# Group norm of the recurrence's outputs by blocks of tokens, within the rounds of the recurrence

## The reference, cut to what matters

```python
_, o = lax.scan(step, state0, (...))             # o: tokens x 8 heads x 64
mu = jnp.mean(o, axis=-1, keepdims=True)
var = jnp.mean(jnp.square(o - mu), axis=-1, keepdims=True)
o = ((o - mu) * lax.rsqrt(var + GN_EPS)).reshape(B, S, D_RWKV) * ln_x_g + ln_x_b
bonus = jnp.sum(rh * kh * r_k, axis=-1, keepdims=True) * vh
o = o + bonus.reshape(B, S, D_RWKV)
return o * g                                     # g = sigmoid(zg) @ w_gate_up
...
mix = jnp.concatenate([attn, rw], axis=-1) @ w_out
x = x + rms_norm(mix, norm_mix_post)
```

## Time and profile before

| | |
|---|---|
| median of three runs | 1931.57 us (1931.26 to 1932.75) |
| profiled execution | 1927.53 us, its span 1925.9 us |
| TensorE (PE) busy | 1806.5 us, 94%; 8894 matmuls |
| VectorE (DVE) busy | 1032.5 us, 54% |
| ScalarE (ACT) busy | 644.4 us, 33% |
| GpSimd (POOL) busy | 84.4 us, 4% |
| DMA | 210.14 MB, mean 109 GB/s |

### The profile page before, as it was taken

The page is one execution under the profiler, slowest core; times in us unless marked ns, Lnnn a source line. Parts: engine busy times, 40 slices in busy tenths (PEclk is TensorE's granted clock), DMA queues, the critical chain, the costliest instruction groups (busy, mean ns, idle before and its releaser), DMA issues. The chain is left out here.

```text
span 1925.9 us, 21538 instructions
## 1 busy us (share of the span) xinstructions
PE 1806.5 (94%) x8894; PEld 1466.7 (76%) x8894; DVE 1032.5 (54%) x1305; ACT 644.4 (33%) x807; POOL 84.4 (4%) x90
## 2 busy tenths in 40 slices
...
PEclk8669999999899899999999999996999999999999
...
GB/s 353 295 73 92 109 249 186 108 153 219 136 85 87 66 109 88 110 88 91 107 92 79 82 109 21 5 23 44 66 99 110 88 99 98 88 109 88 110 88 66
DMA packets 123954, 210.14 MB, mean 109 GB/s; under 512 B 14046, under 2 KB 48502, under 8 KB 123857
## 3 DMA queue, kind: packets, MB, share of 16 engines
...
...
HBM read 205.58 MB, written 4.73 MB: 109 GB/s over the span
## 5 line engine op out<-in xcount | busy, mean ns | idle before, releaser
L1676 DVE TENSOR_TENSOR w_lo<-raw,w_hi 128x2048 fp32r<-128x2048 f32 x138 | 316.3, 2293 | 499.9 <-ACT w_hi L1209 499.9
L1209 ACT ACTIVATE w_hi<-raw 128x2048 fp32r<-128x2048 f32 x138 | 263.8, 1913 | 612.1 <-PE bank L540 584.1
L540 PE MATMUL bank<-h_hi,w_hi 128*128 128x512 f32 x736 | 291.9, 397 | 5.1 <-DVE h_lo L1723 5.1
L540 PE MATMUL bank<-h_lo,w_hi 128*128 128x512 f32 x736 | 288.8, 392 | 0.0
L540 PE MATMUL bank<-h_hi,w_lo 128*128 128x512 f32 x736 | 288.5, 392 | 0.0
L540 PE MATMUL bank<-u_hi,w_hi 128*128 128x512 f32 x512 | 200.7, 392 | 0.0
L540 PE MATMUL bank<-u_hi,w_lo 128*128 128x512 f32 x512 | 199.4, 389 | 0.0
L540 PE MATMUL bank<-u_lo,w_hi 128*128 128x512 f32 x512 | 199.2, 389 | 0.0
L540 PE MATMUL bank<-f_hi,w_hi 128*128 128x512 f32 x496 | 193.0, 389 | 0.0
L540 PE MATMUL bank<-f_lo,w_hi 128*128 128x512 f32 x496 | 193.0, 389 | 0.0
L540 PE MATMUL bank<-f_hi,w_lo 128*128 128x512 f32 x496 | 192.9, 389 | 0.0
...
## 6 DMA issues: line engine op xcount, KB each, us to landing
raw<-in_mlp_w SPq DMA_DIRECT2D x128, 512.0 KB, 4.6
...
```

Of the source, the lines that this page charges most:

```text
L540: mm = te.matmul(bank[:, n], a, b, start=first and k == 0 and j == 0, stop=last and k == 3 and j == 2, skip_group_check=s == SLABS["ffn"] + 1)
L1209: se.activation(m.ring(s)[0], m.raw[:, slot], ACT.Copy).then_inc(sem("hi_made"), 1)
L1676: ve.tensor_tensor(lo, m.raw[:, slot], hi.bitcast(F32), ALU.subtract).then_inc(sem("lo_made"), 1)
```

## The change

The group norm is done by blocks of 128 tokens. The statistics of blocks 0, 1 and 2 are computed by VectorE in rounds 4, 6 and 7 (`O_STATS`: u = 3, 5, 6), square included. GpSimd computes (var/64 + eps)^-0.5 with a multiply-add and a power (`o_rstd`), in place of ScalarE's root and VectorE's reciprocal. In rounds 5, 7 and 8 (`O_BACK`: u = 4, 6, 7) the block is scaled, turned by TensorE (`o_back`) and gated (`o_gated`). Block 3 follows behind the rounds; its transposes stand between the first and the second token block of slab 87.

The bonus moves to round 2 (its products to round 1), the gates to round 3. The algebra is rearranged: `bonus` becomes (bonus + ln_x_b) * gate and `gT` becomes gate * ln_x_g, so that a block needs one multiplication and one addition after it has been turned. `gates()` stands on ScalarE at the end of round 3, behind the exponentials.

The transposes of x stand in round 8 as wide uses, and all eighths of `xT` are done by round 7. `x_before` lies in `kkT` and `vvT` instead of `ar`, and the squares of later norms go to `ar`. `m_hi` and `m_lo` are made by token blocks, slab 86 is split by ScalarE in round 8, and slabs 86 and 87 run one token block after the other, each waiting for its own blocks (`before_tile`). `state(7, 1)` on VectorE is removed.

```diff
-            uses += [("gate", 0), ("gate", 1), ("bonus", 0), ("bonus", 1)]
+        uses += {1: [("bonus", 0), ("bonus", 1)], 2: [("gate", 0), ("gate", 1)], 7: [("x_rows", j) for j in range(4)]}.get(u, [])
+        if u in O_BACK:
+            uses.append(("o_back", O_BACK.index(u)))
...
+O_STATS = (3, 5, 6)
+O_BACK = (4, 6, 7)
+X_FINAL = ((0,), (1,), (2,), (3,), (4, 5), (6,), (7,), ())
...
+        self.o_sq = place_s("o_sq", [P, 512])
...
+            if before_tile and k == 0:
+                before_tile(n)
...
+    def x_to_rows(j):
+        b = wide("x_rows", j)
+        te.wait_ge(sem("x_final"), DT)
+        for k in range(DT):
+            mm = te.transpose(bank[:, b + k // 4, P * (k % 4):P * (k % 4) + P], m.xT[:, k, P * j:P * j + P], ident)
+        mm.then_inc(sem("wide_full"), 1)
...
+    def o_turned(j, b):
+        te.wait_ge(sem("o_scaled"), j + 1)
+        for i in range(4):
+            mm = te.transpose(bank[:, b, P * i:P * i + P], m.o_rows[:, j].rearrange("p h d -> p (h d)")[:, P * i:P * i + P], ident)
+        return mm
...
+        if last:
+            x_to_rows(0)
+            x_to_rows(1)
...
+        if u == 1:
+            bonuses(0)
+            bonuses(1)
+        if u == 2:
             gate(0)
             gate(1)
-            bonuses(0)
-            bonuses(1)
         unit_parts(u)
         if not last:
             key_values(u + 1)
+        else:
+            x_to_rows(2)
+            x_to_rows(3)
         step(u, 0)
+        if u in O_BACK:
+            o_back(O_BACK.index(u))
...
+            def before_tile(n):
+                te.wait_ge(sem("attn_hi" if k == 0 else "o_hi"), n + 1)
+                te.wait_ge(sem("attn_lo" if k == 0 else "o_lo"), n + 1)
+            def last_turned(n):
+                if k == 1 and n == 0:
+                    o_turned(3, 4).then_inc(sem("last_o_turned"), 1)
+            slab(s + k, group, m.m_hi[:, 4 * k:4 * k + 4], m.m_lo[:, 4 * k:4 * k + 4], k == 0, k == 1, None, before_n,
+                 weights_stationary=False, after_n=None if g else last_turned, before_tile=None if g else before_tile)
...
+    def gates():
+        se.wait_ge(sem("inverses_out"), 16)
+        for part in range(2):
+            b = wide_full("gate", part)
+            se.wait_ge(sem("gate_summed"), part + 1)
+            for i in range(2):
+                ins = se.activation(m.gT[:, 2 * part + i], bank[:, b + i], ACT.Copy, scale=m.col("ln_x_g_2", 2 * part + i))
+            ins.then_inc(sem("wide_emptied_act"), 1)
+    def x_rowed(j):
+        b = wide_full("x_rows", j)
+        se.activation(m.x_before[j], bank[:, b:b + 2].rearrange("p b t -> p (b t)"), ACT.Copy).then_inc(sem("wide_emptied_act"), 1)
+    def attn_hi(n):
+        tok = slice(P * n, P * n + P)
+        se.wait_ge(sem("wide_emptied_act"), WIDE_EMPTIED[WIDE_AT["attn", n]][1])
+        se.activation(m.m_hi[:, 0:4, tok], m.attnT[:, :, tok], ACT.Copy).then_inc(sem("attn_hi"), 1)
+    def o_hi(n):
+        tok = slice(P * n, P * n + P)
+        se.wait_ge(sem("o_gated"), n + 1)
+        se.activation(m.m_hi[:, 4:8, tok], m.bonus[:, :, tok], ACT.Copy).then_inc(sem("o_hi"), 1)
...
+        if u == 2:
+            gates()
+        if last:
+            for j in range(4):
+                x_rowed(j)
+            se.wait_ge(sem("attn_summed"), UNITS)
+            split_to(SLABS["w_out"])
+            se.wait_ge(sem("unit_used"), UNITS)
+            for n in range(3):
+                attn_hi(n)
...
+    attn_hi(3)
...
+    for n in range(3):
+        o_hi(n)
+    split_to(SLABS["w_out"] + 1)
+    o_hi(3)
...
+    def bonus_made():
+        ve.wait_ge(sem("blocks_in"), 128)
+        for i in range(4):
+            ins = ve.scalar_tensor_tensor(out=m.bonus[:, i], in0=m.rT[:, i], scalar=m.col("r_k_2", i), in1=m.kkT[:, i],
+                                          op0=ALU.mult, op1=ALU.mult)
+        ins.then_inc(sem("bonus_made"), 1)
...
+    def gates():
+        ve.wait_ge(sem("wide_emptied_dve"), WIDE_EMPTIED[WIDE_AT["bonus", 1]][1])
+        for part in range(2):
+            b = wide_full("gate", part)
+            for i in (2 * part, 2 * part + 1):
+                ins = ve.scalar_tensor_tensor(out=m.bonus[:, i], in0=m.bonus[:, i], scalar=m.col("ln_x_b_2", i), in1=bank[:, b + i % 2],
+                                              op0=ALU.add, op1=ALU.mult)
+            ins.then_inc(sem("gate_summed"), 1)
...
+    def o_stats(j):
+        o, mu, var = m.o_rows[:, j], m.gs[:, 0, j], m.gs[:, 1, j]
+        sq = (m.o_sq[:, :] if j < 3 else m.ar[:, 3, 0]).rearrange("p (h d) -> p h d", h=8)
+        ve.wait_ge(sem("o_copied"), 2 * j + 2)
+        n = own.on(ve.tensor_reduce(mu, o, AX, ALU.add))
+        ve.wait_ge(own.sem, n)
+        n = own.on(ve.tensor_scalar(mu, mu, 1.0 / 64, None, ALU.mult))
+        ve.wait_ge(own.sem, n)
+        n = own.on(ve.tensor_tensor(o, o, spread8(mu), ALU.subtract))
+        ve.wait_ge(own.sem, n)
+        n = own.on(ve.tensor_tensor(sq, o, o, ALU.mult))
+        ve.wait_ge(own.sem, n)
+        ve.tensor_reduce(var, sq, AX, ALU.add).then_inc(sem("o_varied"), 1)
+    def o_scaled(j):
+        ve.wait_ge(sem("o_rstd"), j + 1)
+        ve.tensor_tensor(m.o_rows[:, j], m.o_rows[:, j], spread8(m.gs[:, 1, j]), ALU.mult).then_inc(sem("o_scaled"), 1)
+    def o_gated(j):
+        tok = slice(P * j, P * j + P)
+        ve.wait_ge(sem("wide_emptied_act"), WIDE_EMPTIED[WIDE_AT["gate", 1]][1])
+        if j < 3:
+            b = wide_full("o_back", j)
+        else:
+            b = 4
+            ve.wait_ge(sem("last_o_turned"), 1)
+        ins = ve.tensor_tensor(m.gT[:, :, tok], bank[:, b].rearrange("p (i t) -> p i t", i=4), m.gT[:, :, tok], ALU.mult)
+        if j < 3:
+            ins.then_inc(sem("wide_emptied_dve"), 1)
+            ve.wait_ge(sem("wide_emptied_dve"), WIDE_EMPTIED[WIDE_AT["o_back", j]][1])
+        else:
+            ve.wait_ge(own.sem, own.on(ins))
+        ve.tensor_tensor(m.bonus[:, :, tok], m.bonus[:, :, tok], m.gT[:, :, tok], ALU.add).then_inc(sem("o_gated"), 1)
...
+        for k in X_FINAL[u]:
+            ve.scalar_tensor_tensor(out=m.xT[:, k], in0=m.xT[:, k], scalar=m.col("final_g", k), in1=m.first_rstd,
+                                    op0=ALU.mult, op1=ALU.mult).then_inc(sem("x_final"), 1)
+        if u == 0:
+            bonus_made()
+        if u == 1:
+            bonuses()
+        if u == 2:
+            gates()
+        if u in O_BACK:
+            o_scaled(O_BACK.index(u))
+        if u in O_STATS:
+            o_stats(O_STATS.index(u))
...
+        if u in O_BACK:
+            o_gated(O_BACK.index(u))
...
+    split_to(SLABS["w_out"])
+    for n in range(3):
+        attn_lo(n)
+    o_stats(3)
+    attn_lo(3)
+    for n in range(3):
+        o_lo(n)
+    split_to(SLABS["w_out"] + 1)
+    o_scaled(3)
+    o_gated(3)
+    o_lo(3)
...
+    def o_rstd(j):
+        var = m.gs[:, 1, j]
+        ge.wait_ge(sem("o_varied"), j + 1)
+        ge.tensor_scalar(var, var, 1.0 / 64, GN_EPS, ALU.mult, ALU.add).then_inc(sem("o_meaned"), 1)
+        ge.wait_ge(sem("o_meaned"), j + 1)
+        ge.tensor_tensor(var, var, m.minus_half[:, :], ALU.pow).then_inc(sem("o_rstd"), 1)
     ge.wait_ge(sem("slab_used"), SLABS["w_out"])
     unit_scaled(0)
+    ge.memset(m.minus_half[:, :], -0.5).then_inc(sem("half_set"), 1)
+    ge.wait_ge(sem("half_set"), 1)
     for u in range(1, UNITS):
         unit_scaled(u)
+        if u - 1 in O_STATS:
+            o_rstd(O_STATS.index(u - 1))
+    o_rstd(3)
```

More of the change, by code:

```diff
@@ L518, in emptied, with slab @@
         te.wait_ge(sem(f"{engine}_emptied"), count)
-    def slab(s, group, hi, lo, first, last, before_k=None, before_n=None, weights_stationary=True, k_outer=False, after_n=None):
+    def slab(s, group, hi, lo, first, last, before_k=None, before_n=None, weights_stationary=True, k_outer=False, after_n=None, before_tile=None):
         w_hi, w_lo = m.ring(s)
@@ L1547, in scalar_program @@
             exps(u + 1, (2, 3))
-        else:
-            for part in range(2):
-                b = wide_full("gate", part)
-                se.activation(m.gT[:, 2 * part:2 * part + 2], bank[:, b:b + 2], ACT.Copy).then_inc(sem("wide_emptied_act"), 1)
+        if u == 2:
[8 more added lines that the diff above has]
+                attn_hi(n)
         if u % 2:
@@ new lines, in gates, with spread8 @@
+    def gates():
+        ve.wait_ge(sem("wide_emptied_dve"), WIDE_EMPTIED[WIDE_AT["bonus", 1]][1])
+        for part in range(2):
+            b = wide_full("gate", part)
[3 more added lines that the diff above has]
+            ins.then_inc(sem("gate_summed"), 1)
+    def spread8(a):
+        return a.unsqueeze(2).broadcast_to([P, 8, 64])
@@ L2265, in vector_program @@
         take(u)
-        ve.scalar_tensor_tensor(out=m.xT[:, u], in0=m.xT[:, u], scalar=m.col("final_g", u), in1=m.first_rstd,
-                                op0=ALU.mult, op1=ALU.mult).then_inc(sem("x_final"), 1)
-        if last:
-            for part in range(2):
```

(15 more changed lines are left out.)

117 lines of the change are left out of this document (27 added, 90 removed).

## The result

The changed kernel takes 1904.76 us (median of 4 runs, 1902.13 to 1907.6) where the kernel before takes 1931.41 (median of 4, 1928.64 to 1932.75): a ratio of 0.9874, 95% interval 0.986 to 0.9888. The forecast was 1908.1 with a range of 1903 to 1917. The profiled execution took 1902.54 us with a span of 1900.9, where the kernel before had 1925.9: 25.0 less, against 23.5 forecast.

A forecast was written before the change was run, and what follows sets the result against it. TensorE, busy 94% of the span, was taken as the bound, with time to win only where it stands. The terms summed to -23.45, say -23.5 us, giving a median of 1908.1 us, range 1903 to 1917.

The forecast's parts named there:

- (a): Rounds 2 and 3: the bonus and gate products cost TensorE +7.0 us in full; VectorE's part costs nothing.
- (d): Rounds 5, 7 and 8: `o_back`'s four transposes cost 0.44 us each time, +0.9 for the first two.
- (b): End of round 3: ScalarE's `gates()` behind the exponentials delays the next `probs` by +1.2 us.
- (c): Rounds 4, 6 and 7: a block's norm takes VectorE 3.1 us, fits into 4.14 us of room, costs nothing.
- (e): GpSimd's root: multiply-add and power taken as 1 us a pair (0 to 4.6 kept), at no cost.
- (f): Round 8: loses gates and bonuses, gets the transposes of x; 22.2 us becomes 16.7: -5.5.
- (g): Tail: first w_out product 3.65 us after the last step instead of 31.8: -28.2; nothing late behind it; transposes +0.4.
- (h): Granted clock: loss at the start of w_out unchanged at 1.9 us (-1.9 to +1.9); round 8 +0.5 (0 to 1.6).
- rival that the clock stays up: No clock loss at the start of w_out or in round 8, gate wait shorter by half: -26.5, 1905 us; chance 12%.
- (i): Last w_out group: the 1.28 us table load moves to its first root, +0.25 us on the chain to the next norm.
- VectorE rival: VectorE becomes the bound in rounds 4, 6, 7 and the tail: saving some 15 us, 1917 us; chance 18%.
- slower rival: GpSimd's power is long and delays `kend`: gain gone at D = 17 us a pair, 1940 us at 20; chance 4%.

The follow-up runs named there:

- early gates: Changed kernel with ScalarE's `gates()` called ahead of `key_values(u + 1)` in round 3: 1905.33 us; rounds 2 to 8 take 125.90 instead of 126.99 us.
- repeated squarings: Changed kernel with the squaring of a block in rounds 4, 6 and 7 done five times instead of once: 1916.46 us.
- three squarings: Changed kernel with the squaring of a block in rounds 4, 6 and 7 done three times instead of once: 1907.29 us.
- four more powers: Changed kernel with four more powers of 128x8 on a spare buffer ahead of each root on GpSimd: 1905.84 us.
- five with the waits filled: Changed kernel with five squarings per block and 16 transposes of a constant ahead of TensorE's step in rounds 4, 6 and 7: 1913.66 us.

## Why the prediction was right, step by step

(a) and (d), the work that moved into the rounds: rounds 2 and 3 grew by 3.44 us each (forecast 3.5), rounds 5 and 7 by 0.49 and 0.50 (0.44 each). Right, because TensorE was full there and the costs were rows of the same instructions. The sign given for it, "rounds 2 and 3 of some 20.5 us", missed for round 2, which took 19.52: it had been 16.08 and not 17.0 before.

(b) The gates ahead of `us`: a wait of 0.94 at `probs`, round 4 longer by 1.09 (forecast 1.2). The early gates show that it was theirs. The scaled copies took 0.60 us each, as forecast from 0.69 less 0.1.

(c) The norm of a block: 3.07 us against 3.1, slack 1.17, 0.95 and 0.57. Right, and the repeated squarings show that the edge lies where the rows put it.

(e) The power was mis-sized: 1.64 us instead of less than one (the pair 1.9 instead of 1), as its nearest row was a multiplication. It cost nothing, since 8.8 us would have cost nothing either.

(f) Round 8: 16.69 us against 16.7, with the one wait of 0.31 for `nu` that was foreseen as 0.4. That the number fits is partly luck. The terms that the text gives (7.0 less for gates and bonuses, 1.25 and 0.96 less of waiting, 3.5 more for x, 0.4 for `nu`, 0.6 for ScalarE's copies) make -4.7 and not -5.5, and the third `o_back` (0.44) is in none of them. The trace has no wait for ScalarE's copies, and 0.9 us of the 22.2 before were half clock, which went: these two all but close the gap.

(g) The tail: 3.74 us of waiting, 3.65 forecast. Behind it nothing was late; slab 88's lo part was done at 1334.49 and wanted at 1336.2 (96 products of 0.227 ahead of 1357.98): 1.7 us to spare.

(h) The clock was the weakest term. I took the loss at w_out as unchanged and it was 2.45 and 1.7 us in two traces of the same kernel, against 2.0 before; in round 8, where I had set +0.5, the clock stayed at 1.00, and the 0.9 us that the kernel before loses there was won. The sum came out right as both are small. The median alone, 1904.76, doesn't tell the forecast from the rival that the clock stays up, which named 1905: in round 8 the clock did stay up, at w_out it did not, and there the forecast's 1.9 lies between the two traces.

(i) The table load moved to the first root of w_out's second half, as foreseen. ScalarE and VectorE there, as the earlier trace rows:

```profile
1350.73 1.28 ACT L1618 ACT_TABLE_LOAD   x1
1352.02 0.29 ACT L1618 ACTIVATE row_ms<-row_ms 128x1 f32<-128x1 f32 x1
...
1352.35 0.16 DVE L2411 RECIPROCAL row_ms<-row_ms 128x1 f32<-128x1 f32 x1
```

Counted back from the next norm's first transpose, the reciprocal was 5.87 us ahead of it before and is 5.63 now: late by 0.24, the 0.25 of the forecast. But VectorE had a wait of 0.29 us for ScalarE a few instructions later on this chain, and it has gone; the norm starts no later, and the term was 0. The Trainium skill, "ScalarE: Activation LUTs", section "What ACT_TABLE_LOAD costs", adds a drain of about 1380 ns to the 1283 of the load. The trace has the root 0.01 us behind the end of the load, as it had before, and nothing of a drain.

The median lies 3.3 us under the forecast. Of these 1.05 are the earlier start in the profiled execution, about 0.5 are the stages' own (-24.0 where -23.5 was forecast), and 1.8 come from the step from the one execution to the median: it was 4.0 us above its profiled run before and is 2.2 now, which is scatter.

What did fail is a price that the forecast used but was not put to: "every microsecond of overrun is paid in full", and in the rivals the 15 us and the point D = 17. An overrun is paid in full and then again in clock. The VectorE rival assumed a norm of 4.5 us, which is the kernel with three squarings: rounds 4, 6 and 7 were to pay 1.8 us, and the rounds paid 2.7 (0.9 of them in round 8, behind the wait of round 7). What that rival foresaw for the tail was not tried. For the slower rival the gain was to be gone at 17 us a pair; at 17.6 the kernel is 20 us slower than before, so that point lies between 8.8 and 17.6, and where was not tried.

## What to carry to other kernels

When TensorE is the bound, cut the span at the stretches where it stands, ask which half of the next products does not need what it waits for, and put that half first: here this and what goes with it was two thirds of the gain, and the norm that moved into VectorE's slack the other third. Ask of every wait of TensorE what it costs beyond its length: in these traces half clock behind it cost nothing (behind 0.94 and 1.25 us), mostly 1.4 to 3.1 us, and once 8.2, and the length of the wait alone did not say which. The granted clock in windows of 1 us shows it. Where such a wait can't be removed, transposes of a constant through it to its end, into a bank in which no sum is open, took that second part of its price away.

## What the runs showed of the chip

A wait of 0.71 us was enough for half clock over the next 3.5 us in one place, and waits of 0.94 and 1.25 us left it at full in two others. Waits filled until 0.5 us or less before their end cost no clock; the one of which 2.5 us were left did. The Trainium skill, "TensorE: Matmul & The Clock Gate", section "Why this matters for your kernels", advises against long idle gaps between bursts of matmuls. The traces agree (behind 3.74 us, 1.7 to 2.45 us were lost, and nothing once the gap was filled), and show that one well under a microsecond can count too.

The round ahead of the changed code, round 1, took 14.13 us in three traces and 15.5 to 15.7 in the others, by the same instructions. In three of the latter (four more powers, three squarings, five with the waits filled) the clock fell to half behind its two waits of 1.27 and 0.47 us, and in the three of the former it stayed at 1.00 behind the same two. This and the start of the recurrence differ between traces by 1.6 and 7.4 us, also where every edit lies behind them, and are a part of the scatter of the times.

A power of 128x8 takes GpSimd 1.64 to 1.95 us, nearly three times a multiplication of 128x256 (0.62), and did not slow VectorE beside it: with four more powers a pair the rounds took the same 126.99 us.
